# Dividing the exponents by their sums before they are turned, instead of the finished values

## The chip, the cores and the metric

One core of a Trainium2 chip runs the whole program. The metric is the time of one execution on the device in microseconds (us), as the median of several runs. Engines are named as in the profile: PE is TensorE, DVE is VectorE, ACT is ScalarE, POOL is GpSimd, SP is SyncE.

## The reference

Three transformer layers over one sequence of 512 positions of width 1024. Layer one mixes with causal attention with a decay (12 heads of 64), layer two with latent attention (12 heads, queries and keys of 96), layer three with a sliding window of 128 (8 query heads over 2 key heads, with a sink) and a convolution of 31 taps. Each has four heads of cross attention to 256 memory rows beside it, then an output projection and feed-forward blocks. All attentions share this form (cut):

```python
s = einsum(q, k) * scale                      # masked
m = max(s)                                    # with the sink, where there is one
p = exp(s - m)
w = p / (sum(p) [+ exp(sink - m)])
o = w @ v
```

## The kernel before

Activations lie feature by position (features on the 128 partitions, 512 positions along the row). A dense product takes fp32 data split in two fp32r parts, high and low, and runs as three matmuls of 128x128 by 512 columns (lines 1919 to 1921) or, with positions on the partitions, lines 1937 to 1939. Weights come by DMA, ACT makes the high part (line 2366) and DVE the low part (line 2094).

Attention works on pairs of heads. There are 22 pairs: 2 memory and 6 causal ones in layer one, the same in layer two, 4 windowed and 2 memory ones in layer three. A pair has four row tiles of 128 queries, grouped in units of up to 512 key columns: the causal pairs have units of 128+256, 384 and 512 columns, the windowed ones 128+256 and 256+256, the memory ones twice 256+256. That is 88 row tiles for each of the two heads, in 56 units. For a unit:

- `pscore`: PE forms the scores of both heads in two PSUM banks (lines 2008 to 2025).
- `pmax`: DVE takes the maxima (2190), with the roots of the norm folded in (2199) and the sink (2205).
- `pexp`: ACT takes the exponents of one row tile at a time into an SBUF tile PP, and their sums with the same instruction (2436; the sum is read out by an instruction of its own).
- `pturn`: PE transposes PP, 128 columns at a time, into the score's banks (2037). `pcopya`, `pcopyb`: DVE copies head 0 (2212) and ACT head 1 (2443), or ACT both in the first memory pairs, to SBUF tiles PT.
- `pvals`: PE multiplies by the values into PSUM bank 6 (2051).

At the end of a pair the sums are applied to its finished values. `precip`: DVE adds the sink's exponents (2219) and takes 1/sum for all eight (row tile, head) columns (2222). `pwide`: POOL spreads them over 512 columns (2601). `pbcast`: PE transposes that tile with four instructions (2061). `pspread`: ACT copies it to an SBUF tile F (2459). `pmul`: DVE multiplies bank 6 by F (2227), which frees the bank; ACT makes the high part AOH (2448) and DVE the low part AOL (2230, `pmix`).

The order of work is made in two passes. A generator emits the steps against a clock `now` that counts dense work in beats (one beat is three matmuls of 512 columns). Attention is a side run: `Pairs.run` yields for each unit score(u), then values(u-2), then turn(u-1), and `beat` hands it time at a rate `pace` (0.65 beside the projections of layers one and three, 1.5 elsewhere). `after(n, f)` emits f when `now` has passed n beats more. `Arranged` then replays the steps with estimated durations and lets PE take one of the next 6, DVE and ACT one of the next 5, where it could begin earlier or has more work behind it. Steps of one kind keep their order, and the result is a fixed queue for each engine: an instruction whose input is late holds all behind it.

In layer three DVE also does the convolution: 60 steps of 512 columns in two chains (`tap`, scalar_tensor_tensor on tile RS), then `centre`, `lnscale`, `lnsig`, `lnmul` and `lnlow` (line 2351), which gives chunks 4 and 5 of the mixer's output to the projection. The projection takes the chunks in the order 0, 1, 2, 3, 6, 4, 7, 5.

Of the kernel before, what the change touches and what calls it, by code (L numbers as in the profile page):

```python
# [9 lines left out]
ALU = mybir.AluOpType  # L10
# [481 lines left out]
class Step:  # L492
# [35 lines left out]
    "pwide": ("pwide.pool",),  # L528
    "pbcast": ("pbcast.pe",),
    "pspread": ("pspread.act",),  # L530
    "pmul": ("pmix.mul", "pmix.act"),
# [32 lines left out]
def program(nc, io):  # L564
    with ExitStack() as ctx:
# [471 lines left out]
        class Pairs:  # L1037
# [16 lines left out]
            def score(self, n, u):  # L1054
                job, key, jkey = self.jobs[n], (self.id, n, u), (self.id, n)
                if u == 0:
                    pstats.take(jkey, [("pwide.pool", jkey)])
# [7 lines left out]
                def rest():  # L1065
                    need(job.roots[1] if job.roots else [])
                    for xs in ((slice(0, 2),) if t.joint else (slice(0, 1), slice(1, 2))):
                        step("pmax", key + (xs.start,), job=job, t=t, xs=xs, S=S, tile=key, before=tokens)
                    if job.sealed(u) and job.sink is not None:
                        step("psink", jkey, job=job, S=S, last=key + (0 if t.joint else 1,))  # L1070
                    after(0.8 if job.spare else 0, exponents)

                def exponents():
# [4 lines left out]
                    for x in range(2):  # L1078
                        step("pexp", key + (x,), job=job, t=t, x=x, S=S, P=t.of(PP, t.P, x), before=tokens, src=PS[t.banks[x]],
                             turned=free, top=("pmax.dve", key + (0 if t.joint else x,)))  # L1080
                after(0.4, rest)
                return 0.4 + 1.4 * t.width / 512

            def turn(self, n, u):
                job, key = self.jobs[n], (self.id, n, u)
                need([("pexp.act", key + (1,))])
# [9 lines left out]
                def copies():  # L1096
                    if job.sealed(u):
                        self.recip(n)
# [14 lines left out]
            def values(self, n, u):  # L1113
# [3 lines left out]
                if u == 0:  # L1117
                    psum.take(("pvals", jkey), [("pmix.mul", ckey)], 6)
                step("pvals", key, job=job, u=u, jkey=jkey, t=t)
                return 0.3 * t.width / 128  # L1120

            def sums(self, n, i):

                jkey, ckey = (self.id, n), (self.id, self.jobs[n].chunk)
                need([("pwide.pool", jkey)])
                aux = aux_bank(("pbcast", jkey), [("pspread.act", ckey)])
                step("pbcast", jkey, inv=TMP[tmp.of["inv", jkey]], bank=aux)

                def spread():
                    x = tmp.take(("pmix", ckey), [("pmix.dve", ckey)])  # L1130
                    step("pspread", ckey, jkey=jkey, bank=aux, F=TMP[x], before=tmp.before["pmix", ckey])
                    after(0.1 if self.jobs[n].spare else 0.4, lambda: self.mix(n))
                after(0.3, spread)
                return 0.8

            def recip(self, n):
                job, jkey = self.jobs[n], (self.id, n)
                S = PSTAT[pstats.of[jkey]]
                step("precip", jkey, job=job, S=S, last=self.end(n))
                i = tmp.take(("inv", jkey), [("pbcast.pe", jkey)])  # L1140
                step("pwide", jkey, S=S, inv=TMP[i], before=tmp.before["inv", jkey])

            def mix(self, n):
# [3 lines left out]
                F, h, l = TMP[tmp.of["pmix", key]], AOH[:, job.chunk, :], AOL[:, job.chunk, :]  # L1147
                step("pmul", key, last=self.end(n), F=F, h=h, free=free)
                after(1.2, lambda: step("pmix", key, F=F, h=h, l=l))

            def older(self, scored, turned):

                ends = turned and self.jobs[turned[0]].sealed(turned[1])
                late = ends and self.jobs[turned[0]].spare
                cost = self.sums(*turned) if ends and not late else 0
                cost += self.values(*turned) if turned else 0
                cost += self.turn(*scored) if scored else 0
                return cost + (self.sums(*turned) if late else 0)
# [744 lines left out]
        def tensor(pe):  # L1903
            w = pe if trial(pe) else Once(pe)
            for s in turns(pe, "pe"):
# [125 lines left out]
                elif k == "pturn":  # L2031
                    for t in a["before"]:
                        w.wait_ge(*done(*t))
                    w.wait_ge(*done("pexp.act", key))
# [20 lines left out]
                elif k == "pbcast":  # L2055
                    for t in psum.before["pbcast", key]:
                        w.wait_ge(*done(*t))
                    w.wait_ge(*done("pwide.pool", key))
                    for i in range(4):
                        c = slice(128 * i, 128 * i + 128)  # L2060
                        p = pe.transpose(PS[a["bank"]][:, c], a["inv"][:, c], IDENT)  # L2061
                    p.then_inc(done.sem("pbcast.pe"), 1)
# [15 lines left out]
        def vector(dve):  # L2078
# [6 lines left out]
            for s in turns(dve, "dve"):  # L2085
# [127 lines left out]
                elif k == "precip":  # L2213
                    St = a["S"]
                    for x in range(2):
                        w.wait_ge(*done("pexp.act", a["last"] + (x,)))
                    if a["job"].sink is not None:
                        w.wait_ge(*done("psink.act", key))
                        dve.tensor_tensor(St[:, :, 1, :], St[:, :, 1, :], St[:, :, 2, :],
                                          ALU.add).then_inc(v_in.sem, v_in.up())  # L2220
                        w.wait_ge(v_in.sem, v_in.n)
                    dve.reciprocal(St[:, :, 3, :], St[:, :, 1, :]).then_inc(done.sem("precip.dve"), 1)
                elif k == "pmul":
                    F = a["F"][:, :]
                    w.wait_ge(*done("pvals.pe", a["last"]))
                    w.wait_ge(*done("pspread.act", key))
                    dve.tensor_tensor(F, PS[6][:, :], F, ALU.mult).then_inc(done.sem("pmix.mul"), 1)
# [530 lines left out]
```

## Time and profile before

| | us |
|---|---|
| median of 3 runs (lowest, highest) | 2077.12 (2076.36, 2078.27) |
| profiled execution | 2078.22 |
| its span, first to last instruction | 2076.4 |
| PE, DVE, ACT, POOL busy in the span | 2056.0, 1282.4, 965.0, 50.5 |

The span is what the trace covers; the 1.8 us around it belong to the execution's time. The granted clock was 0.999 of full speed. A row of a group gives its busy time, the mean duration of one instruction and the idle time of the engine before it. Instructions of one engine overlap a little in the records, and matmuls are pipelined, so the distance between two starts is shorter than a duration.

### The profile page before, as it was taken

Reading aid. Unit: us, or ns where it says so; the run is one execution under the profiler, and the core shown is the slowest. Engines: PE = TensorE matmul, PEld = TensorE weight load, DVE = VectorE, ACT = ScalarE, POOL = GpSimd, SP = SyncE. Lnnn points to the kernel's source line nnn. Section 1 sums busy time; section 2 is a strip of 40 time slices with the busy share of each in tenths; the row PEclk is TensorE's granted clock in tenths of the full one; section 3 lists DMA queues with packets and bytes.
Section 4 is the critical chain, followed back from the end, with each engine's and each line's share of the span. In section 5 each row is a group of like instructions: output and inputs, shape, how many; then the busy total and the mean of one; then the engine's idle time right before and its main releaser. Section 6 shows DMA issues by size and latency. Waiting matters only on the chain.

```text
span 2076.4 us, 29986 instructions
## 1 busy us (share of the span) xinstructions
PE 2056.0 (99%) x11114; PEld 1731.9 (83%) x11114; DVE 1282.4 (62%) x2093; ACT 965.0 (46%) x1883; POOL 50.5 (2%) x95
## 2 busy tenths in 40 slices
PE   8999999999999999999999999999999999999999
PEld 8998788888889788888888888888889878888887
DVE  7555588547755877875577544445558985444442
ACT  7655465334446865543344433223344764322331
POOL 0000001000001110000000000000001100000000
PEclk9999999999999999999999999999999999999999
DMA  6222233333333111333333333333332123333332
GB/s 205 62 62 62 62 96 97 98 97 97 96 90 102 35 40 52 102 97 96 97 97 99 97 94 98 98 97 98 98 92 77 37 77 96 97 97 97 98 99 88
DMA packets 101666, 185.53 MB, mean 89 GB/s; under 512 B 11408, under 2 KB 14864, under 8 KB 101264
## 3 DMA queue, kind: packets, MB, share of 16 engines
q1 hardware_dynamic: 101520, 183.61, 30.3%
q8 instruction: 88, 1.44, 0.3%
q14 instruction: 58, 0.48, 0.1%
HBM read 181.47 MB, written 2.10 MB: 88 GB/s over the span
## 4 chain that ended last, share of the span: by engine, by line
PE 94%; DVE 2%; ACT 2%; issue 1%; SPq 0%; DMA 0%; DVEq 0%; ACTq 0%
PE PSA L1919 26%; PE PSA L1921 25%; PE PSA L1920 25%; PE PSA L1937 3%; PE PSA L1938 3%; PE PSA L1939 3%; PE PSA L2025 2%; PE PSA L2051 2%; PE PSA L2037 2%; PE PSA L1979 1%; ACT PP L2436 1%; DVE RS L2082 1%; PE PSA L2008 0%; DVE PSTAT L2190 0%; PE PSA L2061 0%
## 5 line engine op out<-in xcount | busy, mean ns | idle before, releaser
L2366 ACT ACTIVATE WH<-RAW 128x512 fp32r<-128x512 f32 (+2 forms) x681 | 427.0, 627 | 798.1 <-PE PSA L1921 682.0
L2094 DVE TENSOR_TENSOR WL<-RAW,WH 128x512 fp32r<-128x512 f32 (+2 forms) x681 | 468.8, 689 | 394.3 <-ACT WH L2366 369.8
L1919 PE MATMUL PSA<-HNh,WH 128*128 128x512 f32 x1440 | 562.5, 391 | 0.0
L1921 PE MATMUL PSA<-HNh,WL 128*128 128x512 f32 x1440 | 560.3, 389 | 0.0
L1920 PE MATMUL PSA<-HNl,WH 128*128 128x512 f32 x1440 | 560.2, 389 | 0.0
L1920 PEld LDWEIGHTS PSA<-HNl,WH 128*128 128x128 f32 x1440 | 270.3, 188 | 57.1 <-issue 1.2
L1919 PEld LDWEIGHTS PSA<-HNh,WH 128*128 128x128 f32 x1440 | 270.3, 188 | 57.0 <-issue 1.2
L1921 PEld LDWEIGHTS PSA<-HNh,WL 128*128 128x128 f32 x1440 | 270.3, 188 | 56.3
L1919 PE MATMUL PSA<-Gh,WH 128*128 128x512 f32 x704 | 273.9, 389 | 0.0
L1920 PE MATMUL PSA<-Gl,WH 128*128 128x512 f32 x704 | 273.9, 389 | 0.0
L1921 PE MATMUL PSA<-Gh,WL 128*128 128x512 f32 x704 | 273.9, 389 | 0.0
L2117 DVE TENSOR_TENSOR PSA<-PSA,ACC 128x512 f32<-128x512 f32 x180 | 125.5, 699 | 172.4 <-PE PSA L1921 160.3
L1937 PE MATMUL PSA<-WH,HNh 128*128 128x256 f32 (+2 forms) x512 | 153.0, 299 | 8.6 <-DVE HNl L2082 6.4
L1920 PEld LDWEIGHTS PSA<-Gl,WH 128*128 128x128 f32 x704 | 132.1, 188 | 27.5
L1919 PEld LDWEIGHTS PSA<-Gh,WH 128*128 128x128 f32 x704 | 132.1, 188 | 27.5
L1921 PEld LDWEIGHTS PSA<-Gh,WL 128*128 128x128 f32 x704 | 132.1, 188 | 27.4
L1938 PE MATMUL PSA<-WH,HNl 128*128 128x256 f32 (+2 forms) x512 | 147.9, 289 | 0.0
L1939 PE MATMUL PSA<-WL,HNh 128*128 128x256 f32 (+2 forms) x512 | 147.8, 289 | 0.0
L2082 DVE SCALAR_TENSOR_TENSOR CV<-PSA,PAR,CV 128x511 f32<-128x511 f32 (+1 forms) x176 | 131.8, 749 | 11.0 <-ACT CV L2465 2.8
L1937 PEld LDWEIGHTS PSA<-WH,HNh 128*128 128x128 f32 x512 | 98.6, 193 | 11.0 <-DVE HNl L2082 6.4
L1938 PEld LDWEIGHTS PSA<-WH,HNl 128*128 128x128 f32 x512 | 98.9, 193 | 0.2
L1939 PEld LDWEIGHTS PSA<-WL,HNh 128*128 128x128 f32 x512 | 98.6, 193 | 0.0
(267 smaller groups left out, 2253.9 us busy)
## 6 DMA issues: line engine op xcount, KB each, us to landing
RAW<-in_w SPq DMA_DIRECT2D x659, 256.0 KB, 2.6
XT<-in_x SPq DMA_DIRECT2D x8, 256.0 KB, 5.3
MT<-in_mem SPq DMA_DIRECT2D x2, 1024.0 KB, 5.9
out_x<-XT SPq DMA_DIRECT2D x8, 256.0 KB, 2.1
RAW<-in_w SPq DMA_DIRECT2D x8, 208.0 KB, 2.3
RAW<-in_w SPq DMA_DIRECT2D x6, 192.0 KB, 2.3
RAW<-in_w SPq DMA_DIRECT2D x8, 134.0 KB, 5.3
PAR<-in_par SPq DMA_DIRECT2D x1, 207.0 KB, 6.3
```

Source lines behind the costliest of these rows:

```text
L1919: pe.matmul(out, wh, xh, start=(a["start"] and c == 0), stop=False)
L1920: pe.matmul(out, wh, xl, start=False, stop=False)
L1921: p = pe.matmul(out, wl, xh, start=False, stop=ends)
L1937: pe.matmul(out, h[:, c], wh, start=(a["start"] and t % a["share"] == 0), stop=False)
L1938: pe.matmul(out, l[:, c], wh, start=False, stop=False)
L1939: p = pe.matmul(out, h[:, c], wl, start=False, stop=(a["stop"] and t % a["share"] == a["share"] - 1))
L2025: p = pe.matmul(PS[tile.banks[x]][:, col:col + nk], job.q[x][qx][:, qs], job.k[x][kx][:, ks], start=(opens and n == 0 and m == 0), stop=(( ...
L2037: p = pe.transpose(a["out"][:, c], a["P"][:, c], IDENT)
L2082: ins = dve.scalar_tensor_tensor(*x)
L2094: dve.tensor_tensor(l, r, h, ALU.subtract).then_inc(done.sem("split.dve"), 1)
L2117: dve.tensor_tensor(ps, ps, nm.acc, ALU.mult).then_inc(done.sem("scale.dve"), 1)
L2366: act.activation(h, r, ACT.Copy).then_inc(done.sem("split.act"), 1)
```

## The change

The exponents themselves are divided, before PE turns them. For each unit DVE takes the reciprocals of that unit's sums as soon as both heads' exponents are there (`precip`, now once for a unit, as are the sink's exponents and its add). Then DVE multiplies head 0's PP in place (`pscale`) and ACT head 1's (`pscaleb`), one instruction for each row tile. `pturn` waits for these instead of for `pexp`. `pwide`, `pbcast`, `pspread` and `pmul` are gone; ACT and DVE make AOH and AOL straight from bank 6, which is free for the next pair only when `pmix` has ended. The generator counts no cost for the sums any more (0.8 beats a pair before).

```diff
@@ score(self, n, u)
-                    pstats.take(jkey, [("pwide.pool", jkey)])
+                    pstats.take(jkey, [("pscale.dve", self.end(n) + (0,)), ("pscale.act", self.end(n) + (1,))])
...
-                    if job.sealed(u) and job.sink is not None:
-                        step("psink", jkey, job=job, S=S, last=key + (0 if t.joint else 1,))
+                    if job.sink is not None:
+                        step("psink", key, job=job, t=t, S=S, last=key + (0 if t.joint else 1,))
...
+                    after(0.6 + 2.4 * t.width / 512, normed)
+
+                def normed():
+                    step("precip", key, job=job, t=t, S=S)
+                    for x in range(2):
+                        step(("pscale", "pscaleb")[x], key + (x,), t=t, x=x, S=S, P=t.of(PP, t.P, x))
@@ turn(self, n, u)
-                need([("pexp.act", key + (1,))])
+                need([("pscale.act", key + (1,))])
...
-                    if job.sealed(u):
-                        self.recip(n)
@@ values(self, n, u)
-                    psum.take(("pvals", jkey), [("pmix.mul", ckey)], 6)
+                    psum.take(("pvals", jkey), [("pmix.dve", ckey)], 6)
                 step("pvals", key, job=job, u=u, jkey=jkey, t=t)
+                if job.sealed(u):
+                    after(0.5 + 0.3 * t.width / 128, lambda: self.mix(n))
@@ sums(self, n, i) and recip(self, n) are gone; mix(self, n)
-                step("pmul", key, last=self.end(n), F=F, h=h, free=free)
-                after(1.2, lambda: step("pmix", key, F=F, h=h, l=l))
+                step("phigh", key, last=self.end(n), h=h, free=free)
+                after(1, lambda: step("pmix", key, h=h, l=l))
@@ tensor(pe), pturn
-                    w.wait_ge(*done("pexp.act", key))
+                    w.wait_ge(*done(("pscale.dve", "pscale.act")[key[-1]], key))
@@ vector(dve)
-                        w.wait_ge(*done("pexp.act", a["last"] + (x,)))
+                        w.wait_ge(*done("pexp.act", key + (x,)))
...
-                    dve.reciprocal(St[:, :, 3, :], St[:, :, 1, :]).then_inc(done.sem("precip.dve"), 1)
-                elif k == "pmul":
...
+                    dve.reciprocal(St[:, :, 3, rows], St[:, :, 1, rows]).then_inc(done.sem("precip.dve"), 1)
...
+                    dve.tensor_tensor(a["l"], PS[6][:, :], a["h"], ALU.subtract).then_inc(done.sem("pmix.dve"), 1)
+                elif k == "pscale":
+                    w.wait_ge(*done("precip.dve", key[0:3]))
+                    for i, col, k0, nk, masks in a["t"].subs:
+                        P = a["P"][:, col:col + nk]
+                        z = dve.tensor_scalar(P, P, a["S"][:, a["x"], 3, i:i + 1], None, ALU.mult)
+                    z.then_inc(done.sem("pscale.dve"), 1)
@@ scalar(act)
-                elif k == "pmul":
+                elif k == "pscaleb":
+                    w.wait_ge(*done("precip.dve", key[0:3]))
+                    for i, col, k0, nk, masks in a["t"].subs:
+                        P = a["P"][:, col:col + nk]
+                        z = act.activation(P, P, ACT.Copy, scale=a["S"][:, a["x"], 3, i:i + 1])
+                    z.then_inc(done.sem("pscale.act"), 1)
+                elif k == "phigh":
...
+                    act.activation(a["h"], PS[6][:, :], ACT.Copy).then_inc(done.sem("pmix.act"), 1)
```

## Rows read from the trace of the kernel before

**Rows 1.** The page: busy time and instructions; the chain that ended last, by engine

```profile
PE 2056.0 (99%) x11114; PEld 1731.9 (83%) x11114; DVE 1282.4 (62%) x2093; ACT 965.0 (46%) x1883; POOL 50.5 (2%) x95
...
PE 94%; DVE 2%; ACT 2%; issue 1%; SPq 0%; DMA 0%; DVEq 0%; ACTq 0%
```

**Rows 2.** Stretches: length, busy us of PE, PEld, DVE, ACT, POOL; clock, DMA share, GB/s

```profile
52.00:245.00 193.00, 193.00 (x1705) 172.14 (x1705) 113.21 (x213) 110.55 (x290) 4.94 (x8) 1.00 0.20 59
688.00:705.00 17.00, 14.12 (x127) 11.55 (x128) 14.04 (x27) 16.89 (x52) 4.87 (x4) 1.00 0.11 31
705.00:720.00 15.00, 14.00 (x135) 11.45 (x134) 14.16 (x35) 10.43 (x32) 0.62 (x1) 1.00 0.03 5
720.00:825.00 105.00, 105.00 (x758) 87.59 (x756) 78.37 (x141) 66.95 (x170) 8.13 (x11) 1.00 0.16 46
1568.00:1600.00 32.00, 32.00 (x248) 30.94 (x246) 30.40 (x56) 14.86 (x34) 5.29 (x9) 1.00 0.33 91
1600.00:1671.00 71.00, 67.90 (x630) 57.50 (x628) 69.49 (x142) 49.01 (x146) 7.44 (x10) 1.00 0.11 31
1671.00:1692.00 21.00, 20.99 (x142) 15.95 (x140) 18.64 (x32) 16.65 (x35) 1.51 (x2) 1.00 0.22 64
```

**Rows 3.** Groups by line and shape: what goes, and the transposes that stay

```profile
L2037 PE MATMUL PSA<-CONST,PP 128*128 128x128 f32 x392 | 57.7, 280 | 2.1 <-ACT PP L2436 2.1
...
L2227 DVE TENSOR_TENSOR TMP<-PSA,TMP 128x512 f32<-128x512 f32 x22 | 15.1, 688 | 6.7 <-PE PSA L2051 6.1 <-ACT TMP L2459 0.6
...
L2061 PE MATMUL PSA<-CONST,TMP 128*128 128x128 f32 x88 | 13.6, 277 | 0.1
L2459 ACT ACTIVATE TMP<-PSA 128x512 f32<-128x512 f32 x22 | 13.2, 599 | 16.2 <-PE PSA L2061 16.2
...
L2222 DVE RECIPROCAL PSTAT<-PSTAT 128x8 f32<-128x8 f32 x22 | 4.4, 200 | 5.6 <-ACT PP L2436 5.2
```

**Rows 4.** Chain of waits, 1560 to 1720 us: start, us on the chain, engine and line

```profile
1660.12 0.59 PE PSA L2061 x4
...
1673.20 1.02 PE PSA L2037 x8
```

**Rows 5.** Instructions of single lines: ns min/median/max, first and last start

```profile
L2109 DVE COPY ACC<-SQ x7: 417/420/422, 8.2 to 1702.6; 128x512 f32<-128x512 f32 x7
L2109 DVE COPY RS<-SQ x2: 285/286/286, 23.3 to 290.4; 128x256 f32<-128x256 f32 x2
...
L2340 DVE TENSOR_SCALAR HX<-RS,PAR x2: 475/476/477, 1685.4 to 1692.4; 128x512 f32<-128x512 f32 x2
```

**Rows 6.** Groups by line and shape, as rows 3: nearest kinds to what comes

```profile
L2373 ACT ACTIVATE HNh<-XT,PAR 128x512 fp32r<-128x512 f32 x56 | 39.8, 720 | 22.7 <-DVE XT L2082 13.4 <-DVE XT L2236 7.0 <-DMA XT<-in_x 1.9
...
L2380 ACT ACTIVATE SQ<-MT 128x256 f32<-128x256 f32 x16 | 6.3, 403 | 0.0
...
L2112 DVE TENSOR_TENSOR RS<-RS,SQ 128x256 f32<-128x256 f32 x14 | 5.8, 417 | 0.0
...
L2373 ACT ACTIVATE AOH<-MT,PAR 128x256 fp32r<-128x256 f32 x8 | 3.8, 493 | 0.0
```

**Rows 7.** Timeline: start, us from first start to last end, xcount

```profile
701.30 1.28 ACT L2408 ACTIVATE SQ<-YK 128x512 f32<-128x512 f32 x2
...
1613.69 4.14 DVE L2082 SCALAR_TENSOR_TENSOR RS<-HX,PAR,RS 128x512 f32<-128x512 f32 x6
```

**Rows 8.** Timeline, one unit of layer two: its last exponents, then its turn

```profile
749.10 0.68 ACT L2436 ACTIVATE PP<-PSA,PSTAT 128x512 f32<-128x512 f32 x1
...
753.01 1.09 PE L2037 MATMUL PSA<-CONST,PP 128*128 128x128 f32 x8
```

**Rows 9.** Timeline, layer three: first taps; low part of chunk 4; its matmul

```profile
1568.78 5.48 DVE L2082 SCALAR_TENSOR_TENSOR RS<-HX,PAR,RS 128x512 f32<-128x512 f32 x7
...
1691.17 0.69 DVE L2351 TENSOR_TENSOR AOL<-SG,AOH 128x512 fp32r<-128x512 f32 x1
...
1691.91 0.50 PE L1919 MATMUL PSA<-AOH,WH 128*128 128x512 f32 x1
```

More of the change, by code:

```diff
@@ L527 @@
     "precip": ("precip.dve",),
[L528 to L531, printed above, removed]
+    "pscale": ("pscale.dve",),
+    "pscaleb": ("pscale.act",),
+    "phigh": ("pmix.act",),
     "pmix": ("pmix.dve",),
@@ L1146, in mix @@
                 need(free)
-                F, h, l = TMP[tmp.of["pmix", key]], AOH[:, job.chunk, :], AOL[:, job.chunk, :]
-                step("pmul", key, last=self.end(n), F=F, h=h, free=free)
-                after(1.2, lambda: step("pmix", key, F=F, h=h, l=l))
+                h, l = AOH[:, job.chunk, :], AOL[:, job.chunk, :]
+                step("phigh", key, last=self.end(n), h=h, free=free)
+                after(1, lambda: step("pmix", key, h=h, l=l))
             def older(self, scored, turned):
[L1153 to L1158, printed above, removed]
+                cost = self.values(*turned) if turned else 0
+                return cost + (self.turn(*scored) if scored else 0)
             def run(self):
@@ L2054, in tensor @@
                     p.then_inc(done.sem("pvals.pe"), 1)
[L2055 to L2062, printed above, removed]
                 elif k == "centre":
@@ L2443, in scalar @@
                     act.activation(a["dst"], a["src"], ACT.Copy).then_inc(done.sem("pcopy.act"), 1)
-                elif k == "pmul":
+                elif k == "pscaleb":
[5 more added lines that the diff above has]
+                elif k == "phigh":
                     for t in a["free"]:
                         w.wait_ge(*done(*t))
-                    w.wait_ge(*done("pmix.mul", key))
-                    act.activation(a["h"], a["F"][:, :], ACT.Copy).then_inc(done.sem("pmix.act"), 1)
+                    w.wait_ge(*done("pvals.pe", a["last"]))
+                    act.activation(a["h"], PS[6][:, :], ACT.Copy).then_inc(done.sem("pmix.act"), 1)
                 elif k == "psink":
-                    St = a["S"]
+                    St, rows = a["S"], a["t"].rows
                     w.wait_ge(*done("pmax.dve", a["last"]))
                     for x in range(2):
-                        z = act.activation(St[:, x, 2, :], St[:, x, 0, :], ACT.Exp, bias=par("sink", a["job"].sink[x]))
+                        z = act.activation(St[:, x, 2, rows], St[:, x, 0, rows], ACT.Exp, bias=par("sink", a["job"].sink[x]))
                     z.then_inc(done.sem("psink.act"), 1)
-                elif k == "pspread":
-                    for t in a["before"]:
-                        w.wait_ge(*done(*t))
-                    w.wait_ge(*done("pbcast.pe", a["jkey"]))
-                    act.activation(a["F"][:, :], PS[a["bank"]][:, :], ACT.Copy).then_inc(done.sem("pspread.act"), 1)
                 elif k == "conv":
```

33 lines of the change are left out of this document (2 added, 31 removed).

## The prediction, made blind

> **What bounds the kernel now.** I read the page first: PE is busy 2056.0 of 2076.4 us, and 94% of the chain that ended last is PE's [rows 1]. The change takes work from PE and gives more to DVE and ACT, so what matters is which engine is last in each of the three stretches where the 22 pairs run. The table by stage answers that [rows 2]. From 52 to 245 us (layer one, 8 pairs) PE has no gap at all and DVE and ACT are busy 59% and 57%: PE alone. From 688 to 705 us (layer two, memory pairs) ACT is busy 16.89 of 17 us and PE idles 2.9; from 705 to 720 DVE is busy 14.16 of 15 and PE idles 1.0: there the side engines lead, because the next dense product waits for the last queries and keys. From 720 to 825 us PE is alone again. From 1568 to 1671 us (layer three, beside the taps) DVE is busy 99.9 of 103 us, and PE idles 3.1. Last I looked where that stretch hands over: the low part of chunk 4 begins on DVE at 1691.17 and lasts 0.69 us, and the matmul that needs it begins at 1691.91, right behind [rows 9]. So in layer three DVE's queue sets the end of the stretch and PE just keeps step.
>
> **What goes.** `pbcast` is 88 transposes [rows 3]. Their duration overlaps; on the chain eight transposes of the same shape take 1.02 us, so four take 0.51; one block of four shows 0.59 with its change of shape [rows 4]. 22 x 0.51 = 11.2 us leave PE; 13.0 by the dearer row. On DVE `pmul` goes: 0.69 us each, and as instructions overlap (six taps of 0.76 in 4.14 us, so 0.69 each [rows 7]) 0.61 in a full queue, 22 x 0.61 = 13.4 us. On ACT `pspread` goes, 0.60 long and 0.50 in a full queue (two of 0.69 took 1.28 [rows 7]): 11 us. POOL's part fed PE's alone and goes with it.
>
> **What comes on DVE.** 88 tensor_scalars in SBUF. No row shows 128 to 384 columns with a scalar from a column. The nearest: a copy takes 0.286 us at 256 and 0.420 at 512 columns, a tensor_scalar 0.476 at 512 [rows 5]. The copy's slope under the tensor_scalar gives 0.275, 0.34, 0.41 and 0.476 us for 128 to 512 columns, 0.08 less each in a full queue. Bounds for 256: 0.21 (the copy) and 0.34 (a tensor_tensor, 0.417 [rows 6]); I take 0.26, the tensor_scalar being the same kind. A causal pair costs 0.195 + 0.26 + 0.33 + 0.40 = 1.19 us, a windowed one 0.98, a memory one 1.04; all 22 come to 12 x 1.19 + 4 x 0.98 + 6 x 1.04 = 24.4 us. Reciprocals: 56 instead of 22, 34 x 0.20 [rows 3] = 6.8 us; four more adds of the sink, 0.6. Net +18.4 us on DVE.
>
> The Trainium skill ("VectorE: DVE Perf Modes", the section on what auto-detection actually checks) says that a single-source fp32 operation with both ends in SBUF moves two elements a cycle, and its errata table prices it at 58 cycles and half the columns: 0.19 us for 256. The copy's slope agrees (134 ns for 256 columns more), the fixed part does not. By that estimate DVE's share in layer three, below, would be 1.6 us less.
>
> **What comes on ACT.** 88 activations with a scale column: 0.493 us at 256 and 0.720 at 512 columns [rows 6], 0.1 less in a full queue, so 0.28, 0.39, 0.51 and 0.62. The lower bound for 256 is the activation without such a column, 0.403 less 0.1 [rows 6]. A causal pair 1.80, a windowed one 1.45, a memory one 1.56: 36.8 us in all. With `pspread` gone, about +26 us, and a little for the sink's exponents.
>
> **Layer one.** 8 x 0.51 = 4.1 us leave a PE that is alone; DVE and ACT have 80 us of room each [rows 2] and get some 7 and 10 more. The path of a unit grows by a reciprocal and the scale, some 0.2 + 0.8 us with hand-overs 1.5. A typical unit has its last exponent at 749.8 and its turn at 753.0 us [rows 8]: 3.2 us of cover (this one from layer two, at the same distance). Where units have less cover, PE has dense tiles within its reach of 6. `phigh` and `pmix` now hold bank 6 some 0.7 us longer, against the 4 to 6 us until the next pair's values. I take -4.1 us; with the cover gone a unit could cost up to 1 us, bounds -4.7 to +1.
>
> **Layer two.** Six of the eight pairs have their transposes after 720 us: -3.1 us. In 688 to 720 us it goes the other way. Up to 702 us ACT gets the scales of three memory units, 3 x 0.78, and loses one `pspread`: +1.8 us on a full engine. From 702 to 718 DVE gets the scales of four units (0.52 + 0.46 + 0.33 + 0.40) and three reciprocals and loses two `pmul`: +1.1. The next dense product waits behind both, so up to +2.9, and PE's 1.0 us saved there is lost as idle time. I take +2.5, as a little of it falls into gaps; bounds 0 (the planner gives way with scores instead of keys) and +6 (each unit's longer path shows too). Together -0.6 us.
>
> **Layer three.** DVE gets 4 x 0.98 + 2 x 1.04 = 6.0 us of scales, six reciprocals 1.2, four adds 0.6, and loses six `pmul`, 3.7: +4.1 us between 1568 and 1692. The scale's wait stands in DVE's queue behind the reciprocal; behind it are taps and the splits of weights, for which PE waits. The 3.1 us that PE saves cannot show, since it waits for chunk 4 as it is. DVE idles 1.6 + 1.5 + 2.4 = 5.5 us in this time [rows 2], most of it late, when the chain of the normalisation passes between engines; part of that chain's distances can close. If every gap could be used the cost is 0, if none +4.1; I take +3. Upward it reaches +8: scales at the tensor_tensor's rate add 1.3, and since the side run's cost falls by 0.8 beats a pair, taps are emitted some 3 beats later against PE's work, about 2.5 us.
>
> **Sum.** -4.1 - 0.6 + 3 = -1.7 us. The profiled execution took 2078.22 us, 1.8 beside its span; the sum makes it 2076.5. It lay 1.1 above the median of 2077.12, so I put the median of the changed kernel at 2075.4 us. A measurement of this kernel tells 0.2%, 4.2 us, from no change: this is no change.
>
> **Rivals.** *PE's saving arrives whole.* If the planner finds cover in all three stretches, 11.2 us are gone: 2065.9; with one stretch half paid, 2068 to 2072. For it: PE's 99% and the idle 40% of DVE in most of the kernel [rows 1, 2]. Against it: a third of the pairs run where another engine has no room. The Trainium skill ("Perfetto Trace Analysis", Identifying the Most-Contended Engine) says to relieve the engine of highest occupancy first, by which this rival would hold; it adds that the most-contended engine can change between regimes, and the rows by stage show that it does here.
>
> *DVE's queue in layer three pays more than PE saves.* One mechanism: from 1568 us DVE has no room, each reciprocal waits for both heads' exponents and holds the taps behind it, and chunk 4 comes late. With layer one at -4.1 and layer two at +2 (its own queue paying 5), it decides from +6.3 us in layer three; at +8 there the time is 2077.1 - 4.1 + 2 + 8 = 2083. With layer two as forecast it would take +8.9. For it: DVE's 97% and the matmul that begins 0.05 us after its input is through [rows 2, 9]. Against it: DVE's 2.4 us of gaps after 1671, and chunk 5, which has slack.
>
> *The queues come out otherwise.* All orders are planned anew from changed estimates, so the stages could shift by 2 to 3 us each way without any of this. It is spread over the three cases.
>
> **Numbers.** Forecast (within 0.2%, 2073.0 to 2081.3): 0.42. Saving arrives whole or nearly, below 2073.0: 0.33. Layer three pays, above 2081.3: 0.25. The range that leaves 2 in 10 out goes from 2067.0 to 2084.0; the forecast's own is 2073 to 2080.
>
> **What would show it.** PE without L2061 and about 11 us less busy. The stretch in layer two that side engines lead, 688 to 720 us now, would last 34.5 instead of 32 us, with PE idle for 7.4 instead of 3.9. The distance from the first tap, 1568.8, to the low part of chunk 4, 1691.2 [rows 9], would grow from 122.4 to about 125.4 us, with PE's idle time there up from 3.1 to 9. DVE's scale of 256 columns should read 0.34 us and ACT's 0.49. The forecast is wrong if that distance shrinks, or if ACT is not full from 688 to 705 us, or if PE shows new gaps between 60 and 245 us.

## The result: 23 us slower, and the profile after

| | before | after |
|---|---|---|
| median of 4 runs each (lowest, highest), us | 2077.69 (2076.36, 2078.43) | 2100.92 (2099.85, 2102.57) |
| span of the profiled execution, us | 2076.4 | 2098.1 |
| granted clock, mean | 0.999 | 0.994 |

The ratio is 1.0112, with a 95% interval of 1.0099 to 1.0124. The forecast was 2075.4 us, with a range of 2067 to 2084: the sign was wrong, and the time lies 17 us outside.

The page after (busy time by engine; the chain by engine) answers [rows 1]:

```profile
PE 2057.1 (98%) x11026; PEld 1729.0 (82%) x11026; DVE 1299.0 (62%) x2208; ACT 990.5 (47%) x1957; POOL 34.3 (2%) x73
...
PE 90%; DVE 4%; ACT 3%; issue 1%; SPq 0%; DMA 0%; DVEq 0%; ACTq 0%
```

PE has 88 matmuls fewer and yet is busy 1.1 us longer, and 7% of the chain lie on DVE and ACT, where it was 4%. So PE waits where it did not, and it works slower somewhere. (e_none below, which does nothing for the division, has the same 11026 matmuls and is busy 2045.5 us, 10.5 less than before: the forecast's "about 11 us less busy" was right for the work itself.)

**Where: four marks.** The dense work between the attention stretches is the same in both kernels, so the start of an instruction in it tells how late a kernel is there. I take DVE's L2082 on CUM (start of layer one), PE's first and last matmul of the gated units Gh (after layer one; end of the kernel), and the first tap, RS<-HX (start of layer three; 1568.8 before [rows 9]). Rows of single lines, before: count, ns min/median/max, first and last start.

```profile
L2082 DVE SCALAR_TENSOR_TENSOR CUM<-PSA,CUM x2: 681/682/683, 47.1 to 47.8; 12x512 fp32r<-12x512 f32 x2
...
L1919 PE MATMUL PSA<-Gh,WH x704: 389/389/389, 386.8 to 2072.4; 128*128 128x512 f32 x176
```

The same instructions after, where the helper is L2054, and last the low part of chunk 4 (1691.2 before):

```profile
L2054 DVE SCALAR_TENSOR_TENSOR CUM<-PSA,CUM x2: 681/682/683, 47.1 to 47.8; 12x512 fp32r<-12x512 f32 x2
...
L1899 PE MATMUL PSA<-Gh,WH x704: 389/389/389, 387.6 to 2094.0; 128*128 128x512 f32 x176
...
L2054 DVE SCALAR_TENSOR_TENSOR RS<-HX,PAR,RS x60: 721/744/968, 1584.2 to 1688.0; 128x512 f32<-128x512 f32 x60
...
L2324 DVE TENSOR_TENSOR AOL<-SG,AOH x2: 681/684/687, 1711.5 to 1716.4; 128x512 fp32r<-128x512 f32 x2
```

How late each mark is, less how late the one before it is, gives each layer's account: layer one +0.8 us (387.6 - 386.8), layer two +14.6 (1584.2 - 1568.8 less 0.8), layer three +6.2 (2094.0 - 2072.4 less 15.4). The forecast had -4.1, -0.6 and +3. The three misses, 4.9, 15.2 and 3.2 us, make up the whole 23.3 us between forecast and marks; two thirds of them lie in layer two.

**How.** Stretches after, columns as in rows 2:

```profile
52.00:245.00 193.00, 189.82 (x1670) 168.50 (x1669) 118.05 (x251) 118.94 (x314) 0.00 (x0) 1.00 0.20 58
688.00:705.00 17.00, 12.33 (x109) 9.46 (x108) 11.82 (x29) 16.97 (x51) 3.79 (x3) 1.00 0.07 16
705.00:720.00 15.00, 10.49 (x60) 9.05 (x58) 11.49 (x31) 8.45 (x27) 0.00 (x0) 0.58 0.12 36
720.00:735.00 15.00, 12.59 (x90) 10.10 (x90) 9.35 (x23) 8.95 (x21) 0.00 (x0) 0.74 0.00 0
735.00:845.00 110.00, 107.71 (x752) 88.97 (x753) 85.92 (x168) 73.81 (x184) 4.05 (x5) 1.00 0.15 44
707.30:720.90 13.60, 9.77 (x55) 8.53 (x56) 9.76 (x26) 6.15 (x21) 0.00 (x0) 0.50 0.14 40
727.80:734.60 6.80, 6.16 (x36) 5.29 (x35) 3.06 (x11) 3.03 (x7) 0.00 (x0) 0.50 0.00 0
```

Layer three, from the first tap to the low part of chunk 4, before and after:

```profile
1568.80:1691.20 122.40, 119.30 (x1006) 103.26 (x1006) 117.00 (x225) 79.89 (x213) 14.24 (x21) 1.00 0.19 53
```

```profile
1584.20:1711.50 127.30, 116.88 (x975) 99.24 (x975) 121.18 (x259) 86.60 (x239) 8.65 (x15) 1.00 0.17 49
```

PE idles 3.2 us in layer one (0 before [rows 2]), 9.2 us from 688 to 720 (3.9 before) and 10.4 us in the stretch of layer three (3.1 before). In layer two the side engines are not fuller for it: DVE is busy 11.49 of 15 us from 705 to 720 against 14.16. There all three engines wait, in turn, for each other. And for 13.6 and 6.8 us the granted clock reads 0.50, the 1.2 GHz level, after PE had been busy 12.33 of 17 us; before the change it stayed at 1.00 there. In layer three DVE has 4.2 us more work and the stretch is 4.9 us longer.

PE's longer waits that the kernel before did not have, over the whole span (line, releaser: us in all, times, longest):

```profile
PE PSA L2017 <- DVE PP L2202: 11.3, 10, 1.7
...
PE PSA L2005 <- ACT PT L2416: 4.6, 4, 2.2
PE PSA L1899 <- DVE XT L2209: 2.6, 3, 1.2
PE PSA L2031 <- DVE AOL L2197: 2.3, 1, 2.3
```

L2017 is the turn, L2202 the new scale on DVE. One turn in full, that of the third memory unit of layer two (start, length; in brackets the idle time before and its releaser):

```profile
699.07 0.63 ACT L2409 ACTIVATE PP<-PSA,PSTAT,QR 128x256 f32<-128x256 f32 x1
...
702.23 1.28 ACT L2381 ACTIVATE SQ<-YK 128x512 f32<-128x512 f32 x2
703.03 0.69 DVE L2094 TENSOR_REDUCE SS<-SQ 128x8 f32<-128x512 f32 x1 [3.88 <-ACT SQ L2381]
703.63 0.17 DVE L2194 RECIPROCAL PSTAT<-PSTAT 128x4 f32<-128x4 f32 x1
703.83 0.62 DVE L2202 TENSOR_SCALAR PP<-PP,PSTAT 128x256 f32<-128x256 f32 x2
704.29 0.89 ACT L2421 ACTIVATE PP<-PP,PSTAT 128x256 f32<-128x256 f32 x2
...
704.60 0.63 PE L2017 MATMUL PSA<-CONST,PP 128*128 128x128 f32 x4 [0.80 <-DVE PP L2202]
```

The last exponents and the read-out of their sum end at 699.8 us. The reciprocal, 0.17 us of work, stands behind a tensor_reduce, and this waits 3.88 us for ACT's squares. DVE is idle meanwhile, and the turn comes 4.8 us after the exponents. PE stands idle for 3.0 us of these: 2.16 us for a copy by ACT (L2416) and 0.80 us in front of this turn.

### The profile page after: what moved, and what is told of

Read it like the earlier page. It is cut to its first block, busy times and chain, and to the rows that moved or that the text cites. A ratio compares the mean times of both kernels' runs of the same rounds, so it can differ in the third digit from the quotient of the medians.

```text
span 2098.1 us, 30061 instructions
## 1 busy us (share of the span) xinstructions
PE 2057.1 (98%) x11026; PEld 1729.0 (82%) x11026; DVE 1299.0 (62%) x2208; ACT 990.5 (47%) x1957; POOL 34.3 (2%) x73
## 4 chain that ended last, share of the span: by engine, by line
PE 90%; DVE 4%; ACT 3%; issue 1%; SPq 0%; DMA 0%; DVEq 0%; ACTq 0%
PE PSA L1899 25%; PE PSA L1901 25%; PE PSA L1900 25%; PE PSA L1917 3%; PE PSA L1918 3%; PE PSA L1919 3%; PE PSA L2031 2%; PE PSA L2005 2%; PE PSA L2017 2%; ACT PP L2409 1%; DVE PSTAT L2162 1%; DVE RS L2054 1%; PE PSA L1959 1%; PE PSA L1988 0%; PE PSA L1998 0%
## 5 line engine op out<-in xcount | busy, mean ns | idle before, releaser
L2089 DVE TENSOR_TENSOR PSA<-PSA,ACC 128x512 f32<-128x512 f32 x180 | 125.4, 699 | 171.2 <-PE PSA L1901 159.2
L2054 DVE SCALAR_TENSOR_TENSOR CV<-PSA,PAR,CV 128x511 f32<-128x511 f32 (+1 forms) x176 | 131.8, 749 | 11.0 <-ACT CV L2439 3.0
```

What stands on the lines that cost most here:

```text
L2054: ins = dve.scalar_tensor_tensor(*x)
L2089: dve.tensor_tensor(ps, ps, nm.acc, ALU.mult).then_inc(done.sem("scale.dve"), 1)
```

## The experiments

All medians were taken beside runs of the kernel before on the same chip. The layer columns come from the four marks, each in one profiled execution (less the shift at the first mark, -1.5 to +0.8 us), so a difference of 1 us between them tells little.

| kernel | median, us | ratio (95%) | layer 1 | 2 | 3 |
|---|---|---|---|---|---|
| e_none: no reciprocals, no scales | 2071.31 | 0.9971 (0.9960 to 0.9982) | -3.9 | -1.0 | -2.4 |
| e_undiv: reciprocals alone | 2077.6 | 1.0000 (0.9990 to 1.0009) | -3.9 | +2.9 | +0.1 |
| e_load_a: with ACT's scales, unwaited for | 2076.4 | 0.9994 (0.9984 to 1.0003) | -3.6 | +1.5 | +1.0 |
| e_load_d: with DVE's scales, unwaited for | 2082.13 | 1.0021 (1.0012 to 1.0031) | -3.6 | +1.9 | +6.4 |
| e_load2: with both, unwaited for | 2088.08 | 1.0047 (1.0032 to 1.0062) | -3.6 | +3.7 | +8.5 |
| the changed kernel | 2100.92 | 1.0112 (1.0099 to 1.0124) | +0.8 | +14.6 | +6.2 |
| e_early: scales further forward | 2095.03 | 1.0080 (1.0065 to 1.0095) | +0.9 | +7.9 | +7.9 |
| e_early_r: and the reach 9, 7, 7 | 2089.33 | 1.0053 (1.0038 to 1.0068) | -2.2 | +7.2 | +5.6 |
| e_heads: a reciprocal for each head | 2106.0 | 1.0135 (1.0118 to 1.0152) | -0.1 | +15.2 | +13.7 |
| e_pool: second head on POOL | 2110.52 | 1.0154 (1.0139 to 1.0169) | +5.6 | +18.4 | +8.9 |
| e_bank: bank 6 freed by a copy | 2102.19 | 1.0121 (1.0106 to 1.0137) | +1.7 | +17.9 | +8.7 |
| e_warm: 10 idle transposes at 10 units | 2100.82 | 1.0115 (1.0098 to 1.0132) | +0.8 | +15.5 | +7.5 |
| e_warm2: 12 at 5 units | 2099.58 | 1.0108 (1.0093 to 1.0123) | +0.8 | +13.2 | +7.3 |
| b_cost4: before, pair's cost 0.4 | 2076.48 | 0.9997 (0.9988 to 1.0006) | +0.1 | -0.1 | -1.0 |
| b_r: before, reach 9, 7, 7 | 2077.72 | 1.0001 (0.9992 to 1.0010) | +0.1 | 0.0 | -0.6 |
| h1_r: division in layer one alone | 2075.37 | 0.9989 (0.9980 to 0.9998) | -2.2 | -0.2 | -0.6 |

Two things stand behind the layer columns. The profiled execution of e_bank is the slowest of its four, 4.3 us above their median. And in layer three the granted clock stays at 1.00 in the kernel before, the changed one, e_none, e_undiv, e_load_a and e_early_r, but reads 0.50 for some 3 us in e_early, e_pool and e_bank and for some 7 us in e_load_d, e_load2, e_heads, e_warm and e_warm2. Their last column may hold up to half of that besides what the edit does. This is an estimate: in the changed kernel the same sixteen matmuls of a unit's values take 1.97 us at 0.50 and 1.09 us at 1.00.

**No scales.**

```
-  need([("pscale.act", key + (1,))])
+  need([("precip.dve", key)])
-  w.wait_ge(*done(("pscale.dve", "pscale.act")[key[-1]], key))
+  w.wait_ge(*done("pexp.act", key))
```

> The changed kernel without the scales: sums and reciprocals are formed, nothing is divided (the attention values stay undivided, which is left out of the computation), and a turn waits for the exponents alone. Theory A (the 24 us are the scale between exponents and turn: its wait, its load, or both): PE has lost 88 transposes and nothing stands in their place, so 2064 to 2070 us, PE idle from 688 to 720 us back to about 4 us, and no stretch at the half clock beside the one at 24 us. Rival D (the new order of emission or the longer hold of bank 6 costs the time, not the scale): 2085 us or more.

2077.6 us: between the two. The scales cost 23 us, so the rival that put it all on order and bank falls; but a turn that waits on the chip for nothing new still brings no gain, where 2064 to 2070 were expected. Its marks, to be read beside the changed kernel's:

```profile
L2052 DVE SCALAR_TENSOR_TENSOR RS<-HX,PAR,RS x60: 719/744/949, 1568.1 to 1665.4; 128x512 f32<-128x512 f32 x60
...
L1897 PE MATMUL PSA<-Gh,WH x704: 389/389/389, 383.2 to 2071.8; 128*128 128x512 f32 x176
```

Layer one gives its 3.9 us in full. Layers two and three give none. Its stretch from 688 to 705 us, beside PE's 14.12 before [rows 2], shows PE busy less and not done sooner, and a clock of 0.88 (half speed for a part of it), which theory A had excluded:

```profile
688.00:705.00 17.00, 12.58 (x105) 10.62 (x103) 12.15 (x30) 14.54 (x45) 3.77 (x3) 0.88 0.12 32
```

**The load without the wait.** The first head's scale writes TMP[1] and the second's TMP[2]; PE waits for the exponents. Two small waits come in with it: each scale waits for the last one on its engine, and an exponents' tile is given back only when its scale has read it. And a turn is emitted when the exponents are, where e_undiv emits it only after the unit's reciprocal.

```
-  z = dve.tensor_scalar(P, P, ...)
+  z = dve.tensor_scalar(TMP[1][:, col:col + nk], P, ...)
-  z = act.activation(P, P, ACT.Copy, ...)
+  z = act.activation(TMP[2][:, col:col + nk], P, ACT.Copy, ...)
```

> The changed kernel with its scales writing to scratch tiles, each engine one behind the other: VectorE and ScalarE carry the whole load of the scales, and PE's turn waits for the exponents alone (so the division is left out of the result). The kernel without scales took 2077.6 us, so the scales cost 23 us. Theory A1 (most of these are the series exponents, reciprocal, scale, turn): 2078 to 2086 us. Rival A2 (they are the load on two engines that have no room): 2093 to 2101 us.

2088.1 us, 2 above the one window and 5 below the other: 10.5 us of the 23 are load, 12.8 the wait. By the marks the load falls on layer three (8.4 of it), and the wait on layers one (4.4) and two (10.9), with 2.3 given back in layer three, where this run has its 7 us at half clock and the changed kernel none.

```profile
L2054 DVE SCALAR_TENSOR_TENSOR RS<-HX,PAR,RS x60: 720/746/948, 1569.7 to 1676.0; 128x512 f32<-128x512 f32 x60
...
L1899 PE MATMUL PSA<-Gh,WH x704: 389/389/389, 384.0 to 2081.8; 128*128 128x512 f32 x176
```

**Whose load.** `for x in range(1)` and `for x in range(1, 2)` in place of `range(2)` around the two scales.

> As the kernel whose scales go to scratch tiles (2088.1 us; the division left out of the result), but with VectorE's scales alone and none on ScalarE. Against the kernel without scales the load of both cost 8.3 us in layer three, 0.8 in layer two, 0.3 in layer one. Theory D (VectorE's queue feeds the convolution taps and is full in layer three, as the prediction has it): all but about 1 us of the 8.3 stays, 2085 to 2089 us. Rival E (ScalarE's scales delay what VectorE waits for): 2078 to 2082 us.

> The mirror of it: ScalarE's scales to scratch and none on VectorE (the division left out). Theory D: 2077 to 2080 us. Rival E: 2084 to 2089 us. If each alone costs little and both together 10 us, the two cost jointly, which neither theory has.

2082.1 us with DVE's alone is 3 us below D's window and at the upper edge of E's; 2076.4 us with ACT's alone is 0.6 below D's and 8 below E's. So neither number of D was met, but the pair tells the engine: against e_undiv DVE's scales cost 6.3 us in layer three and ACT's 0.9 (by the medians, 4.5 and -1.2 over the whole kernel). E falls on its second number. 1.2 us come only with both. From first tap to chunk 4, e_undiv and then DVE's scales alone:

```profile
1568.10:1689.80 121.70, 116.21 (x978) 99.82 (x977) 115.33 (x238) 78.95 (x216) 9.30 (x15) 1.00 0.18 53
```

```profile
1566.20:1694.10 127.90, 118.69 (x977) 101.66 (x977) 121.82 (x262) 78.48 (x216) 10.15 (x15) 0.97 0.17 50
```

DVE is busy 6.5 us more and the stretch is 6.2 us longer, with 6.4 and 6.1 us of DVE's idle time in it: the engine was as full without the scales, and the half clock in the second row adds nothing that shows.

**Place in the queue.** `after(0, normed)` in place of `after(0.6 + 2.4 * t.width / 512, normed)`.

> The changed kernel with reciprocal and scales emitted together with the exponents instead of 0.6 + 2.4 x width/512 beats later, so they stand further forward in the queues of VectorE and ScalarE. In the trace of the changed kernel the reciprocal of the fourth memory unit has its exponents at 699.8 us and runs at 703.63, behind a tensor_reduce that waits for ScalarE's squares. Theory Q (the place in the in-order queue makes the long waits): that distance falls below 1 us and the time is 2088 to 2097 us. Rival R (a forward place makes VectorE wait for exponents with taps and splits behind it): 2101 us or more.

2095.0 us, 5.9 less. The same unit as above, now:

```profile
699.50 0.62 ACT L2409 ACTIVATE PP<-PSA,PSTAT,QR 128x256 f32<-128x256 f32 x1
...
700.32 0.18 DVE L2194 RECIPROCAL PSTAT<-PSTAT 128x4 f32<-128x4 f32 x1 [0.80 <-ACT PP L2409]
```

The reciprocal follows the exponents at once (the expectation calls the unit the fourth; by the order of the turns it is the third); the 3.88 us behind the squares are gone from it. Layer two gains 6.7 us, so theory Q holds there. Layer three loses 1.7. DVE does wait for exponents twice in it, 1.27 and 1.11 us, but behind the last tap, and the distance from first tap to chunk 4 grows by 0.4 us only; so R's mechanism, taps held up, is not shown, and this run has its 3 us at half clock there.

**A reciprocal for each head.** `step("precip", key + (x,))`, waiting for `pexp.act` of that head.

> The changed kernel with a reciprocal for each head, which waits for that head's exponents alone, so the first head's scale can run beside the second head's exponents. VectorE gets 56 more instructions of 0.17 us. If the series at each unit is the cost, the first turn comes up to 0.8 us earlier at the units without cover: 2092 to 2098 us. Rival (the second head's end sets the unit, or queue places do): 2099 to 2106 us.

2106.0 us, 5 slower, at the upper edge of the rival's window. Layer one gains 0.9, as the series would have it. Layer three loses 7.5 for 12 more reciprocals and 8 more adds of the sink, some 3 us of DVE's time; PE's waits for a scale in front of a turn go from 3.4 to 9.3 us there. The rest may be queue places or the 7 us at half clock of this run; the two are not told apart.

**The second head on POOL.** `pool.tensor_scalar` in place of `act.activation`.

> The changed kernel with the second head's scale on POOL instead of ScalarE. ScalarE loses some 36 us of work, above all from 688 to 705 us where it is full. If ScalarE's load is what delays layer two: 2088 to 2096 us. Rival: POOL takes 1 us or more for a scale and the turn waits for it: 2105 us or more.

2110.5 us, the rival's. POOL's scale (group by shape: busy, mean ns, idle before it):

```profile
L2569 POOL TENSOR_SCALAR PP<-PP,PSTAT 128x256 f32<-128x256 f32 x48 | 52.8, 1106 | 110.4 <-DVE PSTAT L2194 110.4
```

1.11 us where ACT takes 0.51 and DVE 0.35. Six tenths of a microsecond more in the series go with 4.8 us in layer one and 3.8 in layer two, although ACT is busy 33 us less. That is the series' price once more, from the other side.

**Bank 6.** DVE copies it to SBUF after the last values; the high and low part are made from the copy.

```
+  dve.tensor_copy(a["F"][:, :], PS[6][:, :]).then_inc(done.sem("pmix.mul"), 1)
```

> The changed kernel, but VectorE first copies bank 6 to SBUF and the high and low part are made from the copy, so that bank 6 is given back one operation after the last values, as before. VectorE gets 22 copies of about 0.5 us. Theory B (the next pair's values waiting for the bank is a main cause): 5 us or more below 2101, and PE's wait for the low part at 711 us gone. Rival A: that wait is 2.3 us of the 24, and the copies cost some of it in layer three: 2097 to 2103 us.

2102.2 us, in rival A's window. PE's longest waits from 688 to 735 us:

```profile
PE PSA L2017 <- DVE PP L2207: 8.9, 4, 5.0
```

The wait for AOL is gone and its time stands at the turn instead (5.3 us in the changed kernel from 688 to 735 us; this is the slowest execution of e_bank). Theory B falls.

**The clock.** Twelve transposes of IDENT into the unit's own bank, ahead of the wait for the scale (ten of them, at ten units, in the first run).

> The changed kernel with ten idle transposes of the identity ahead of the turn of each unit of layer two's first four pairs, after the exponents and before the wait for the scale, into the bank that the turn then overwrites: PE works where it waited. Theory C (the granted clock falls to the 1.2 GHz level at 707 us because PE had idled, and its 20.5 us there cost up to 10 us): the clock reads 1.0 from 690 to 740 us and the time is 2090 to 2096 us, or the transposes take back a part, 1.3 us a unit where nothing was waited for. Rival (the clock follows something else, or half speed is hidden by the waits): clock as low as before or time at 2101 us or above.

> The changed kernel with twelve idle transposes of the identity ahead of the turns of five units only, the four memory units of layer two and the second unit of the first causal pair, between their exponents and their scales. With ten at each of ten units the stretch at the half clock from 707 us went to a few us, and the time stayed at 2100.8. Theory C1 (the half clock costs 4 to 8 us and the other run paid them back in idle transposes at units without a wait): 2093 to 2097 us. Rival C2 (PE's slow work lies beside VectorE's and ScalarE's series there, which set the time): clock about 1.0 and 2099 to 2103 us.

2100.8 and 2099.6 us, against 2100.9: the first at the edge of the rival's window, the second in C2's. Stretches of the second run, to be read beside the changed kernel's 1.00, 0.58 and 0.74:

```profile
688.00:705.00 17.00, 15.63 (x139) 12.91 (x139) 12.50 (x29) 15.94 (x48) 3.81 (x3) 1.00 0.12 33
705.00:720.00 15.00, 9.13 (x76) 7.58 (x71) 11.77 (x31) 9.54 (x30) 0.00 (x0) 0.89 0.05 17
720.00:735.00 15.00, 13.32 (x118) 10.79 (x118) 10.77 (x25) 10.52 (x27) 0.00 (x0) 1.00 0.05 15
```

Most of the half clock of layer two is gone (3 us of it are left), and 1.3 us come back, no more than the executions of one kernel differ (2099.85 to 2102.57 us for the changed one). Its timeline shows why; after it comes the line of the changed kernel for the same unit, the fourth memory unit's turn:

```profile
715.37 1.12 PE L2024 MATMUL PSA<-CONST,PP 128*128 128x128 f32 x4 [4.76 <-DVE PP L2209]
```

```profile
715.02 3.22 PE L2017 MATMUL PSA<-CONST,PP 128*128 128x128 f32 x14 [1.49 <-DVE PP L2202]
```

At full clock PE was done 3 us sooner and then stood 4.76 us for the same scale. In layer two the slow clock was paid beside a wait that was there anyway: C2 holds for it. For layer three these runs say nothing, since both have 7 us at half clock there.

**No reciprocals either.** The step `precip` is dropped from e_undiv.

> The changed kernel with neither reciprocals, sink terms nor scales (all that divides is left out of the computation). The kernel with reciprocals but without scales took 2077.6 us, 3 us later in layer two than before and equal in layer three. Theory G (the 56 reciprocals and the sink terms, with VectorE waiting for exponents behind them, cost the saving): layer two falls to -2 or lower and the whole to 2068 to 2072 us. Rival H (the stretch from 688 to 720 us and layer three are led by other engines, so PE's saving does not arrive there): layer two at +1 to +3, the whole at 2074 to 2078 us.

2071.3 us, inside G's window; against e_undiv 6.3 us. But layer two stands at -1.0 where G wanted -2 or lower. So both hold in part: with nothing to do for the division, 7.3 of the 11.2 us arrive by the marks, 6.1 by the medians. Not all of the 6.3 us need be the reciprocals': e_undiv also emits each turn later, after its reciprocal, and e_load_a, which has the reciprocals and ACT's scales but not that, is at +1.5 in layer two where e_undiv is at +2.9. This run too idles from 688 to 705 us, as the first row shows; its marks follow.

```profile
688.00:705.00 17.00, 12.52 (x107) 10.03 (x103) 11.26 (x28) 14.84 (x46) 3.77 (x3) 0.90 0.17 48
```

```profile
L2052 DVE SCALAR_TENSOR_TENSOR RS<-HX,PAR,RS x60: 741/745/950, 1562.5 to 1655.4; 128x512 f32<-128x512 f32 x60
...
L1897 PE MATMUL PSA<-Gh,WH x704: 389/389/389, 381.5 to 2063.7; 128*128 128x512 f32 x176
```

Where its idle time lies says more. A tensor_reduce of layer two's norms waits for ACT's squares, the copy of head 0 (L2182) stands behind it on DVE, and PE waits for the copy:

```profile
694.24 0.55 DVE L2092 TENSOR_REDUCE SS<-SQ 128x4 f32<-128x384 f32 x1 [4.15 <-ACT SQ L2379]
...
697.96 0.68 DVE L2182 COPY PT<-PSA 128x512 f32<-128x512 f32 x1
...
698.78 0.70 PE L2003 MATMUL PSA<-UQH 96*128 96x128 f32 x4 [3.37 <-DVE PT L2182]
```

DVE's waits for these squares from 683 to 712 us, before and in this run (us in all, times, longest):

```profile
DVE SS L2122 <- ACT SQ L2408: 0.3, 1, 0.3
```

```profile
DVE SS L2092 <- ACT SQ L2379: 4.7, 2, 4.1
```

They are 4.6 us in e_undiv, 3.3 to 5.5 in the three load runs and 4.1 in the changed kernel. So this wait comes with the new order of the queues and not with the division; in the changed kernel a reciprocal happened to stand behind it.

**The side run's cost.** `return 0.4` in place of `return 0.8` in `sums`.

> The kernel before with the cost that the spreading of a pair's sums reports to the side run at 0.4 instead of 0.8 beats; nothing else is changed and every instruction stays. The changed kernel reports none. If the emission order shifted by this is part of the loss: 2080 us or more. Otherwise within 2 us of 2077.5.

2076.5 us: no difference that can be told. The beats are not the cause, at least by half.

**The planner's reach.** `{"pe": 9, "dve": 7, "act": 7, "pool": 1}` in place of 6, 5, 5.

> The kernel with reciprocal and scales emitted with the exponents (2095.0 us), with the planner's reach widened from 6, 5, 5 steps to 9, 7, 7 on PE, VectorE and ScalarE. If the waits left are a matter of order in the queues: layer one falls to between -4 and -2 us against the kernel before and the whole to 2082 to 2090 us. If the series itself binds where no other work is ready: 2092 to 2097 us.

> The kernel before with the planner's reach 9, 7, 7 instead of 6, 5, 5 on PE, VectorE and ScalarE. Control for the run in which the same widening took the changed kernel with early scales from 2095.0 to 2089.3 us. If the widening only gives back what the series of waits cost: 2075 to 2079 us. If it helps any order of this kernel: 2070 to 2074 us.

2089.3 and 2077.7 us. With the division the wider reach is worth 5.7 us, in the kernel before nothing. So part of the series' cost was a lack of other work within reach of PE: layer one goes from +0.9 to -2.2, layer three from +7.9 to +5.6. Layer two moves by 0.7 only. DVE no longer waits for the squares there, yet 6.6 us of PE's waits from 685 to 845 us lie in front of a turn, 6.1 of them for a scale (1.4 before the change, for exponents):

```profile
PE PSA L2017 <- DVE PP L2202: 6.1, 4, 2.4
```

So in layer two the series has its cost without that wait, too.

**Layer one alone.** `self.new = self.id in (0,)` chooses between the two kernels' code, with early scales and the wider reach.

> The kernel before in layers two and three and the changed one, with early scales, in layer one, both with reach 9, 7, 7. Layer one stood at -2.2 us with these in the other run, where VectorE and ScalarE have 40% of room. If each layer's account is its own: 2.2 us below the kernel before with the same reach, about 2075 us. If the neighbours in the queues matter across layers, anywhere else.

2075.4 us, as expected; of the kernels that compute everything it is the fastest, 2.0 us under the one before and 2.35 under it with the same reach, with an interval that ends at 0.9998: a gain just above what can be told. The layers' accounts add up. Its first and last mark (the first tap is at 1567.0):

```profile
L2106 DVE SCALAR_TENSOR_TENSOR CUM<-PSA,CUM x2: 681/682/682, 47.7 to 48.4; 12x512 fp32r<-12x512 f32 x2
...
L1943 PE MATMUL PSA<-Gh,WH x704: 389/389/389, 385.2 to 2070.0; 128*128 128x512 f32 x176
```

## Why the prediction was wrong, step by step

**Durations: right.** The groups by shape, mean ns behind the bar:

```profile
L2421 ACT ACTIVATE PP<-PP,PSTAT 128x256 f32<-128x256 f32 x48 | 22.6, 512 | 3.6 <-DVE PSTAT L2194 3.6
...
L2202 DVE TENSOR_SCALAR PP<-PP,PSTAT 128x256 f32<-128x256 f32 x48 | 15.2, 347 | 0.2
```

0.347 and 0.512 us against 0.34 and 0.49. The counts (88, 88, 56) were right too, and so was the load: DVE is busy 16.6 us more and ACT 25.5, against 18.4 and 26. No cost of an operation was mis-sized; what failed is what an operation's time costs where it stands.

**Layer two, 688 to 720 us: the step that failed.** "The next dense product waits behind both, so up to +2.9 ... bounds 0 and +6 (each unit's longer path shows too)." The prediction summed the added work on two engines and kept the longer path as an outer bound. It was the other way round: by the end of the layer the kernel is 14.6 us late, of which 2.9 are there without scales, 0.8 is their load (e_load2 against e_undiv) and 10.9 the wait. The stretch was read as one in which ACT is full. It is one in which PE, ACT and DVE hand a unit round; that no dense product is ready to fill it is argued, from the planner's wider reach that brought 0.7 us there. Seven units turn between 688 and 735 us, and at the prediction's own 1.5 us of longer path each they make 10.5 us, an estimate that fits the 10.9. The place in the queue is a part of it: moving the steps forward gave 6.7 us back. The test named for it, PE idle 7.4 instead of 3.9 us from 688 to 720, came out at 9.2; "ACT full from 688 to 705" was met (16.97), and from 705 on DVE was emptier, not fuller. The 22 reciprocals of this layer, 3.4 us of DVE's time in e_undiv, go with 3.9 us between e_none and e_undiv, a part of which is the later emission of the turns.

**Layer one: failed, inside its bounds.** "3.2 us of cover" for a path of 1.5 more. The saving is real (-3.9 us without scales) and the load is free (-3.6 with it), but the wait takes 4.4 us. The 3.2 us were one unit's [rows 8], from layer two, and far from the shortest. The last unit of layer one before the change, its second head's exponents and its turn:

```profile
234.51 0.69 ACT L2436 ACTIVATE PP<-PSA,PSTAT 128x512 f32<-128x512 f32 x1
...
235.22 1.09 PE L2037 MATMUL PSA<-CONST,PP 128*128 128x128 f32 x8
```

It has 0.02 us of cover. The +0.8 measured lies just inside the upper bound of +1, where the forecast took -4.1. "New PE gaps between 60 and 245 us", the sign named for a wrong forecast, are there: 3.2 us.

**Six later pairs of layer two: failed in part.** PE idles 2.3 us from 735 to 845 and the transposes' 3.1 us are mostly given back.

**Layer three: right in kind, half in size.** DVE's queue does set it. The term was +3 of +4.1, the rest falling into gaps; measured were +6.2. The distance from first tap to chunk 4 went from 122.4 to 127.3 us (1584.2 to 1711.5), for 125.4 forecast, with PE idle 10.4 us in it for 9 forecast. DVE's work in it grew by 4.2 us, as forecast; but its idle time, which was to take up 1.1 of them, grew from 5.4 to 6.1. DVE's scales alone show the same: 6.0 us of forecast work costs 6.3, so none of it fell into a gap. The other 1.3 us come after chunk 4's low part has begun, and no run tells why. That the series came 2.3 us cheaper than the unwaited load (+6.2 against +8.5) may be the half clock that only the latter has in this layer; this isn't tested.

**Bank 6: small.** 0.7 us against 4 to 6 of slack was wrong once: PE waited 2.3 us for the low part. Freeing the bank gained nothing.

**The rivals.** "The saving arrives whole" was not reached even with no division at all: 7.3 us arrive. The slower rival named layer three, where it took +8 and 6.2 came, and allowed layer two 2 us where 14.6 came. Even the three upper bounds together, +1, +6 - 3.1 and +8, end 12 us above the kernel before; no rival had the series of waits as its mechanism. It stood in the prediction as a bound only ("with the cover gone", "each unit's longer path shows too"). "The queues come out otherwise", a shift of 2 to 3 us each way, did happen: DVE's wait for the squares, and e_none's missing 2 us in layer two.

**What stays open.** Whether another order would bring the 2 us between e_none's layer two (-1.0) and the 3.1 us of saving that were forecast there; the 3.37 us that PE waits behind the squares point to it, but no run moves that step. Further the joint 1.2 us of both loads in layer three, and how much of the columns of layer three is the half clock.

## What to carry to other kernels

Before adding a step between a producer and the turn that waits for it, find the stretches in which the engines hand work round, and charge the step there at full length for each unit, plus what can stand ahead of it in an in-order queue. Look up the cover of every unit, not of a typical one. Moving work off the busiest engine paid 1.0 us of 3.1 where engines hand work round (layer two of e_none). A kernel that leaves the step out, and one that does it without the wait, tell load from latency in two runs; look in both for waits that only the new order brings, and at the granted clock of each stretch that you compare.

## What the runs showed of the hardware that was not expected

The granted clock fell to 0.50, the 1.2 GHz level, for 13.6 and 6.8 us, after PE had been busy 12.33 of 17 us; it stayed at 1.00 before the change, with 14.12 of 17 [rows 2]. Bringing it back in layer two gained at most 1.3 us. The Trainium skill ("TensorE: Matmul & The Clock Gate", HAM oscillation — how this bites in real kernels) prices throttled time at half its length; by that the 20.4 us would be worth some 10 us, an estimate from its rule. The run with the clock back at 0.89 to 1.00 does not bear this out here, since PE then waited 4.76 us for a scale. It is not free everywhere: the four executions of e_bank, one program, took, sorted, 2100.95, 2101.56, 2102.82 and 2106.53 us with mean granted clocks of 0.997, 0.997, 0.994 and 0.993. From first to last that is some 17 us more at half clock (an estimate: twice 0.004 of 2104 us) and 5.6 us more time.

POOL's scale of 256 columns by a column of scalars takes 1.11 us, of 512 columns 2.0 us, against 0.35 and 0.49 on DVE. The Trainium skill ("GPSIMD Engine Reference", Engine selection) calls one-input work on this engine roughly line-rate; the row speaks against it for this operation, by a factor of 3 against DVE. (Spans on POOL are rough in the profile; two such scales together took 1.91 to 2.37 us.)
